# One weight product of a decoder layer computed as seven block products per pair of output tiles

## The reference

```
h  = rmsnorm(x) ; z = h @ W_in                          # values, gates, q, k, v
c  = silu(layernorm(causal_conv31(val * sigmoid(glu))))
ya = ((c @ w_pw) * silu(c_gate)) @ w_br_conv            # convolution branch
yb = (attention(q, k, v) * silu(a_gate)) @ w_br_attn    # attention branch
m  = sigmoid(g_conv) * ya + sigmoid(g_attn) * yb
x  = x + rmsnorm(m @ w_out) ; x = x + sigmoid(x @ w_pg) * (p @ w_pp)
```

## Time and profile before

| | |
|---|---|
| median of 3 runs (1166.1 to 1166.4) | 1166.13 us |
| span of the profiled execution | 1164.1 us |
| median above that span | 2.0 us |
| PE busy | 1158.8 us, 100% |
| DVE busy | 856.9 us, 74% |
| ACT busy | 377.5 us, 32% |

### The profile page before, as it was taken

One profiled execution on the slowest core, in us unless ns is written; L12 is line 12 of the kernel. 1 busy time (PEld: TensorE's weight loads), 2 busy tenths in 40 slices (PEclk: granted clock), 3 DMA queues, 4 the chain that ended last, 5 costly groups with the idle time before them and its releaser, 6 DMA issues.

```text
span 1164.1 us, 16101 instructions
## 1 busy us (share of the span) xinstructions
PE 1158.8 (100%) x6304; PEld 945.5 (81%) x6304; DVE 856.9 (74%) x961; ACT 377.5 (32%) x671; POOL 18.0 (2%) x16
## 2 busy tenths in 40 slices
PE   9999999999999999999999999999999999999998
PEld 7888888888888888877777888888888888888887
DVE  6999999999999984699986688683233344357776
ACT  6431221221221221366665442441112112344342
POOL 2020000000000000000000000000000000000000
PEclk9999999999999999999999999999999999999999
DMA  9622122122222323211112111333232232434565
GB/s 352 274 90 72 60 84 72 63 81 72 67 78 72 100 54 86 54 56 56 58 56 77 50 55 37 108 108 96 85 108 92 88 108 81 136 113 141 174 205 180
DMA packets 35675, 116.42 MB, mean 100 GB/s; under 512 B 4496, under 2 KB 5264, under 8 KB 35632
## 3 DMA queue, kind: packets, MB, share of 16 engines
q1 hardware_dynamic: 25264, 82.29, 21.3%
q10 hardware_dynamic: 10368, 33.56, 8.3%
HBM read 92.10 MB, written 20.97 MB: 97 GB/s over the span
## 4 chain that ended last, share of the span: by engine, by line
PE 97%; DVE 1%; ACT 1%; DMA 0%; issue 0%; SPq 0%; ACTq 0%; DVEq 0%
PE psg L470 81%; PE psg L762 6%; PE psg L494 2%; PE psb L676 1%; PE psg L733 1%; PE psg L577 1%; PE psg L523 1%; PE psg L694 1%; ACT probs L1009 1%; PE psg L728 1%; PE psb L577 1%; PE psg L819 0%; DMA p_raw<-pT 0%; DVE smax L1471 0%; DVE probs L1495 0%; DVE probs L1465 0%
## 5 line engine op out<-in xcount | busy, mean ns | idle before, releaser
L470 PE MATMUL psg<-h_hi,w_hi 128*128 128x512 f32 x768 | 236.9, 390 | 0.0
L470 PE MATMUL psg<-h_hi,w_lo 128*128 128x512 f32 x768 | 236.5, 389 | 0.0
L470 PE MATMUL psg<-h_lo,w_hi 128*128 128x512 f32 x768 | 236.4, 389 | 0.0
L1213 DVE TENSOR_TENSOR w_lo<-w_raw,w_hi 128x1024 fp32r<-128x1024 f32 x113 | 138.1, 1222 | 89.1 <-ACT w_hi L865 85.4
L865 ACT ACTIVATE w_hi<-w_raw 128x1024 fp32r<-128x1024 f32 x112 | 118.5, 1058 | 250.4 <-PE psg L470 230.7
L470 PEld LDWEIGHTS psg<-h_hi,w_lo 128*128 128x128 f32 x768 | 144.1, 188 | 30.1
L470 PEld LDWEIGHTS psg<-h_hi,w_hi 128*128 128x128 f32 x768 | 143.8, 188 | 30.4 <-issue 0.8
L470 PEld LDWEIGHTS psg<-h_lo,w_hi 128*128 128x128 f32 x768 | 144.1, 188 | 30.0
L1390 DVE SCALAR_TENSOR_TENSOR conv<-u,cols,conv 128x1024 f32<-128x1024 f32 x120 | 154.1, 1284 | 0.0
L1390 DVE SCALAR_TENSOR_TENSOR work<-u,cols,work 128x1024 f32<-128x1024 f32 x112 | 145.5, 1300 | 0.0
L762 PE MATMUL psg<-h_hi,w_hi 128*128 128x512 f32 x128 | 51.8, 405 | 0.0
(11 more groups left out here) (257 smaller groups left out, 1763.2 us busy)
## 6 DMA issues: line engine op xcount, KB each, us to landing
w_raw<-weights SPq DMA_DIRECT2D x114, 512.0 KB, 3.4
gates<-ring ACTq DMA_DIRECT2D x24, 512.0 KB, 2.7
ring<-gates ACTq DMA_DIRECT2D x24, 512.0 KB, 3.4
x_rows<-x_rows SPq DMA_DIRECT2D x8, 512.0 KB, 10.1
conv<-xT SPq DMA_DIRECT2D x8, 512.0 KB, 14.3
ple<-ple_out SPq DMA_DIRECT2D x8, 512.0 KB, 13.5
x_ring<-xT ACTq DMA_DIRECT2D x16, 256.0 KB, 3.5
ple_all<-ple ACTq DMA_DIRECT2D x8, 512.0 KB, 4.7
```

Of the source, the lines that this page charges most:

```text
L470: mm = nc.tensor.matmul(psg[:, slot, h * HALF:(h + 1) * HALF], w[:, wslot, (wk + k) * P:(wk + k + 1) * P], r[:, k, h * HALF:(h + 1) * HALF ...
L1213: nc.vector.tensor_tensor(w_lo[:, slot, :], w_raw[:, slot, :], w_hi[:, slot, :].bitcast(F32), ALU.subtract).then_inc(w_lo_ready, 1)
```

## The change

F's numbers vanish and G, H, I move down by eight (`G0` = 66). The product `c @ w_pw` is done for four **pairs** of output tiles. For a pair the operands are seen as 2 x 2 blocks: `c` by halves of the features (4 row tiles) and halves of the 1024 columns, the weights by halves of the features and the two output tiles. Plain multiplication takes eight block products, each of 4 k-steps x 3 passes = 12 matmuls of 128x512. The new code uses Winograd's form with seven, named P1, P2, P6, Q5, P7, Q3, P4 in the order in which PE does them (`seventh`). It needs

- four sums of blocks of `conv` (`row_sum`, s blocks 0 to 3), each 128x2048, with their high part (`sum_high`, ACT) and low part (`row_low`, DVE), once for all pairs;
- per pair four sums of weight blocks (`pair_sum`, DVE, 128x512), and for each of the seven products a high part (`block_high`, ACT) and a low part (`block_low`, DVE), in six slots of `pair_w`, which lie over `w_raw`, `w_hi` and `w_lo`;
- per pair four copies out of PSUM (`keep`, ACT): P6, P7, Q3 and P4 are added onto a bank that holds earlier products, so PE waits for the copy (`kept_ready`) before it goes on there;
- per pair four quarters of the result (`take`, DVE): an add or subtract and a product with the gate, all of 128x512 (the last of them the product alone). Rows of y are then split after the third pair (`y_high`, `y_low`).

The s blocks lie over `o_lo` and `o_hi`, which PE reads until the end of tile 65; `o_used` frees them in quarters. `merged` is no longer kept in SBUF: DVE writes each row to `merged_out` (`merge_row`), ACT sends it to memory (`spill_merged`), and SP loads the eight rows back during the last pair and after (`merged_back`). The normalisation is done by the fifth E tile that DVE reads out (`norm_beside`).

Core of the diff (`...` marks what is left out):

```diff
-            return ((0,), (1, 2), (3,), (4, 5), (6,), (7,), (), ())[m]
+            return ((0, 1), (2,), (3, 4), (5,), (6, 7), (), (), ())[m]
...
+            sp.wait_ge(product_made, LAST_PAIR)
+            load_tile(G0)
...
+            for k in range(4):
+                merged_back(k)
+            sp.wait_ge(product_made, LAST_PAIR + 7)
+            load_tile(G0 + 1)
+            for k in range(4, KT):
+                merged_back(k)
...
-            pairs(F0, G0, c_hi, c_lo, 2 * KT)
...
+            def seventh(i, n):
+
+                b = 7 * i + n
...
+                pe.wait_ge(pair_lo, b + 1)
...
+                if i == 0 and n in (P6, P7, Q3):
+                    pe.wait_ge(s_ready, {P6: 2, P7: 3, Q3: 4}[n])
...
+                if onto:
+                    pe.wait_ge(kept_ready, 4 * i + {P6: 1, P7: 2, Q3: 3, P4: 4}[n])
...
+            block_high(0)
+            block_high(1)
+            sum_high(0)
+            sum_high(1)
+            block_high(2)
+            sum_high(2)
+            block_high(3)
+            keep(0, P1)
+            sum_high(3)
+            block_high(4)
+            block_high(5)
+            keep(0, P6)
+            keep(0, Q5)
+            block_high(6)
+            load_gate(KT + 1, 1, G0 // 2)
+            spill_merged(KT - 1)
+            for b in range(7, 7 * PAIRS):
+                for i, n in made_since(b):
+                    if n in (P1, P6, Q5, P7) and 7 * i + n > Q5:
+                        keep(i, n)
...
+                block_high(b)
+            y_high(0)
+            y_high(1)
+            keep(PAIRS - 1, P7)
+            high(G0 // 2 - 1, 2)
+            for k in range(2, KT):
+                y_high(k)
+            high(G0 // 2 - 1, 3)
...
+                if n < 3:
+                    dve.wait_ge(o_used, n + 1)
...
+                nc.vector.tensor_tensor(s_raw[:, n], a, b, op).then_inc(s_made, 1)
```

More of the change, by code:

```diff
@@ L55 @@
 E0 = 58
[L56 to L61, removed]
+G0 = 66
+H0 = 74
+I0 = 90
+TILES = 106
+WTILES = 90
+PAIRS = KT // 2
+KP = KT // 2
+P1, P2, P6, Q5, P7, Q3, P4 = range(7)
+LAST_PAIR = 7 * (PAIRS - 1)
 PLE_STEPS = 2
@@ L134, in build @@
         w_lo = at("w_lo", [2, KT * P], F32R, W + 16 * KB)
+        pair_w = at("pair_w", [6, 2, HALF], F32R, W)
+        pair_t = at("pair_t", [6, 2, HALF], F32, W)
         tanh_t = at("tanh_t", [S], F32, G)
@@ L346, in norm_beside, with pair_slot, slot_before, pair_bank @@
         def norm_beside(m):
-            return ((0,), (1, 2), (3,), (4, 5), (6,), (7,), (), ())[m]
+            return ((0, 1), (2,), (3, 4), (5,), (6, 7), (), (), ())[m]
+        def pair_slot(b):
+            r = b % 6 if b < LAST_PAIR else 3 + (b - LAST_PAIR) % 3
+            return 2 * r if r < 3 else 2 * (r - 3) + 1
+        def slot_before(b):
+            if b < 6:
+                return None
+            return b - 6 if b < LAST_PAIR + 3 else b - 3
+        def pair_bank(i, n):
+            return {P2: 2, Q5: 3, Q3: 3}.get(n, i % 2)
+        def made_since(b):
+            first = 2 if b == 7 else slot_before(b - 1) + 1
+            return [divmod(c, 7) for c in range(first, slot_before(b) + 1)]
+        def from_slot(eng, b):
+            if b < 6:
+                eng.wait_ge(tile_done, G0 - 1 + KT + (b >= 3))
+            else:
+                eng.wait_ge(product_made, slot_before(b) + 1)
         block = ctx.enter_context(nc.Block())
@@ L799, in _ @@
             pairs(D0 + 6, E0, h_hi, h_lo)
-            pairs(E0, F0, o_hi, o_lo, KT)
-            pairs(F0, G0, c_hi, c_lo, 2 * KT)
+            pairs(E0, G0 - 2, o_hi, o_lo, KT)
+            tile(G0 // 2 - 1, 0, o_hi, o_lo)
+            pe.wait_ge(w_lo_ready, G0 - 1 + PLE_STEPS + 1)
+            pe.wait_ge(ps_free[1], G0 // 2 + 3)
+            for k in range(KT):
+                for n, (w, r) in enumerate(((w_hi, o_hi), (w_lo, o_hi), (w_hi, o_lo))):
+                    for h in range(2):
+                        mm = nc.tensor.matmul(psg[:, 1, h * HALF:(h + 1) * HALF], w[:, 1, k * P:(k + 1) * P],
+                                              r[:, k, h * HALF:(h + 1) * HALF],
+                                              start=(k == 0 and n == 0), stop=(k == KT - 1 and n == 2))
+                if k % 2 == 1 and k < KT - 1:
+                    mm.then_inc(o_used, 1)
@@ L802, in _ @@
+            for i in range(PAIRS):
+                for n in range(7):
+                    seventh(i, n)
             pairs(G0, H0, y_hi, y_lo, 3 * KT)
@@ L1118, in _ @@
                 load_gate(m, j, a2)
+                if m >= 2:
+                    spill_merged(m - 2)
                 if m == 0:
@@ L1124, in _ @@
                         c_high(k - 1)
-                high(a2, j + 2)
-                if m == KT - 1:
+                if m < KT - 2:
+                    high(a2, j + 2)
+                if m == 5:
                     c_high(KT - 1)
[L1128 to L1135, removed]
+            load_gate(KT, 0, G0 // 2)
+            spill_merged(KT - 2)
+            block_high(0)
[18 more added lines that the diff above has]
+                        keep(i, n)
+                    if n == P1 and i > 0:
+                        act.wait_ge(y_made, 4 * i)
+                        for j in range(2):
+                            act.dma_start(ring[:, j, :], GATES[:, KT + 2 * i + j, :]).then_inc(gate_loaded[j], 16)
+                block_high(b)
[6 more added lines that the diff above has]
+            high(G0 // 2 - 1, 3)
+            act.wait_ge(y_made, 4 * PAIRS)
             with act.Fori(0, KT // 2) as i:
@@ L1628, in gate, with merge_row, pair_sum @@
                 dve.wait_ge(gate_loaded[j], r * 16)
-            for m in range(KT):
+            def merge_row(m):
                 a2, j = (E0 + m) // 2, m % 2
+                gate(a2, j, m // 2 + 1)
+                if m >= 2:
+                    dve.wait_ge(merged_spilled[j], 16 * (m // 2))
+                stt(merged_out[:, j, :], ring[:, j, :], 1.0, psg[:, j, :], ALU.add, ALU.mult).then_inc(ps_free[j], 1)
+            def pair_sum(i, n):
+                blocks = pair_raw[i % 2]
+                dve.wait_ge(pair_loaded[i % 2], 16 * (i // 2 + 1))
+                if n == Q5:
+                    out, a, b = pair_sums[:, 0, :], blocks[:, 0, :], blocks[:, 1, :]
+                elif n == P6:
+                    dve.wait_ge(pair_summed, 4 * i + 1)
+                    out, a, b = pair_sums[:, 1, :], pair_sums[:, 0, :], blocks[:, 3, :]
+                elif n == P4:
+                    from_slot(dve, 7 * i + n)
+                    out, a, b = pair_t[:, pair_slot(7 * i + n), 1, :], pair_sums[:, 1, :], blocks[:, 2, :]
+                else:
+                    from_slot(dve, 7 * i + n)
+                    out, a, b = pair_t[:, pair_slot(7 * i + n), 1, :], blocks[:, 1, :], blocks[:, 3, :]
+                nc.vector.tensor_tensor(out, a, b, ALU.add).then_inc(pair_summed, 1)
@@ new lines, in _, with row_sum @@
+            upper, lower = slice(0, HALF), slice(HALF, S)
+            def row_sum(n):
+                a11, a12 = conv[:, 0:KP, upper], conv[:, KP:, upper]
+                a21, a22 = conv[:, 0:KP, lower], conv[:, KP:, lower]
+                if n < 3:
+                    dve.wait_ge(o_used, n + 1)
+                else:
+                    dve.wait_ge(tile_done, G0 + KT)
+                if 0 < n < 3:
+                    dve.wait_ge(s_made, n)
+                a, b, op = ((a21, a22, ALU.subtract), (s_raw[:, 0], a11, ALU.subtract),
+                            (a12, s_raw[:, 1], ALU.add), (a11, a21, ALU.subtract))[n]
+                nc.vector.tensor_tensor(s_raw[:, n], a, b, op).then_inc(s_made, 1)
@@ new lines, in row_low, with take @@
+            def row_low(n):
+                dve.wait_ge(s_hi_ready, n + 1)
+                stt(s_lo[:, n], s_raw[:, n], 0.5, s_hi[:, n].bitcast(F32), ALU.mult, ALU.subtract).then_inc(s_ready, 1)
+            def take(i, n):
+                m, half = ((2 * i, upper), (2 * i + 1, lower), (2 * i + 1, upper), (2 * i, lower))[n]
+                dve.wait_ge(product_made, 7 * i + (P2, P7, Q3, P4)[n] + 1)
+                if n > 0 or i > 0:
+                    dve.wait_ge(y_made, 4 * i + n)
+                if n < 3:
+                    dve.wait_ge(kept_ready, 4 * i + (1, 4, 2)[n])
+                    a, b, op = ((psb[:, pair_bank(i, P2), :], kept[:, 0, :], ALU.add), (kept_q5[:], kept[:, 0, :], ALU.subtract),
+                                (psb[:, pair_bank(i, Q3), :], kept[:, 1, :], ALU.subtract))[n]
+                    nc.vector.tensor_tensor(quarter[:], a, b, op).then_inc(quarter_read, 1)
+                    dve.wait_ge(quarter_read, 3 * i + n + 1)
+                dve.wait_ge(gate_loaded[m % 2], (i + 5) * 16)
+                nc.vector.tensor_tensor(y_raw[:, m, half], quarter[:] if n < 3 else psb[:, pair_bank(i, P4), :],
+                                        ring[:, m % 2, half], ALU.mult).then_inc(y_made, 1)
@@ L1632, in _, with y_low @@
+            def y_low(k):
```

(61 more changed lines are left out.)

133 lines of the change are left out of this document (119 added, 14 removed).

## The result

The changed kernel takes 1169.14 us (median of 11 runs, 1168.2 to 1170.5) against 1166.20 of the kernel before: a ratio of 1.0024 with an interval of 1.0016 to 1.0032, slower by 0.24%. The profiled execution has a span of 1167.3 us, 3.2 more than before.

The account below looks back on a forecast made before the run. PE's list of matmuls was taken to bound the kernel. -10.9 + 0.1 + 1.5 + 0.1 + 5.2 + 2.9 = -1.1 us gave a span of 1163.0, with 2.0 for the median 1165.0 us; range 1161.8 to 1169.5.

Parts of the forecast that it names:

- What is removed: In the product done in pairs, 48 fewer matmuls at 0.2266 us each: 10.9 us less on PE.
- The prices: Costs of added operations, such as 2.28 us on DVE and 1.92 us on ACT for 128x2048.
- The entry: From tile 65's end to P4 of pair 0: PE loses 0.1, 1.5 (before P7), 0.1 and 5.2 us (before P4).
- The exit: From the last product to tile 66: PE waits 2.9 us for the low part of tile 66's weights.
- Steady state: Second to fourth pair: DVE's 11.7 and ACT's 6.9 us hide beside PE's 19.0 us per pair; no loss.
- normalisation: In E, done in five tiles instead of eight: DVE's 46.7 of 54.4 us, hidden.
- merged rows: Eight spills and eight loads of 512 KB share the DMA engines; DVE waits for them, nothing reaches PE.
- The sum: Over the whole kernel, the gain and PE's waits add to -1.1 us: span 1163.0, time 1165.0 us.
- the forecast's own case: Whole kernel with entry and exit waits as worked out: 1165.0 us, bounds 1163.2 to 1167.7, chance 63%.
- the clock falls: Rival: idle of 5.2 us before P4 drops PE's clock to 1.2 GHz, giving 1167.7 to 1170.5 us; chance 12%.
- a falling clock as a sign of being wrong: Behind the copy keep(0, P7) before P4: the forecast is wrong if the granted clock falls after it.
- 11 were named as a sign: Whole kernel: PE's busy time lower by 11 us, with 48 fewer matmuls, would show the forecast right.

Follow-up runs that it names:

- Run 1: Changed kernel with the copy of P7 (pair 0) right behind ACT's last high part of pair 0 and take(0, 0) before row_low(3) on DVE: 1166.39 us.
- Run 2: Changed kernel with high and low part of tile 66's weights moved ahead of y_high(0) and y_low(0): 1164.72 us.
- run 4: Changed kernel with thrown-away matmuls on PE, 20 before P4 of pair 0 and 10 before tile 66: 1165.27 us.
- run 7: Kernel before, with PE held ahead of tile 66 (first of F) while GpSimd fills a free tile five times: 1174.66 us.
- run 8: Kernel before, with PE held ahead of tile 66 (first of F) while GpSimd fills a free tile twice: 1170.67 us.
- run 3: Changed kernel with the moves of run 1 and Run 2 together: 1162.97 us.
- run 6: Changed kernel with only the 20 thrown-away matmuls before P4 of pair 0, the wait before tile 66 left in: 1166.63 us.
- run 5: Changed kernel with the moves of run 1 and Run 2, plus ACT's copy of P1 (pair 1) before the high part of that pair's P7: 1159.55 us.

## Why the prediction was wrong, point by point

**What is removed, 10.9 us: right.** Outside the waits and the slow stretches, 21 products take 57.16 us, 0.2269 us per matmul.

**The prices: right.** In the trace after, the 128x2048 operations take 2.29 us on DVE and 1.92 to 1.93 on ACT, where 2.28 and 1.92 were estimated. Here is ACT at the entry, with the copy of P7 at 832.99:

```profile
817.82 1.92 ACT L1262 ACTIVATE s_hi<-s_raw 128x2048 fp32r<-128x2048 f32 x1 [2.08 <-DVE s_raw L1881]
...
828.69 0.33 ACTq L1225 DMA_DIRECT2D ring<-gates  x1
829.05 0.46 ACTq L1245 DMA_DIRECT2D merged<-merged_out  x1
829.61 1.15 ACT L1257 ACTIVATE pair_w<-pair_raw 128x512 fp32r<-128x512 f32 x2 [2.81 <-DVE merged_out L1836]
832.45 0.63 ACT L1257 ACTIVATE pair_w<-pair_sums 128x512 fp32r<-128x512 f32 x1 [1.70 <-DVE pair_sums L1853]
832.99 0.58 ACT L1272 ACTIVATE kept<-psb 128x512 f32<-128x512 f32 x1
```

**The entry: right.** 0.1 us lost before P6 (forecast 0.1), 1.3 before P7 (1.5), 5.3 before P4 (5.2), by the steps that were named. The chain is the one forecast: gate load behind the read-out of tile 65, three high parts, the last behind two sums, then the copy. Run 1 confirms the cause and adds what the prediction didn't say: ACT's list holds a second copy of this kind, P1 of pair 1, hidden behind the first.

**The exit: right.** 2.9 us lost (2.9). DVE has two y_low at 890.27 and two at 893.60, then the `take` in two operations, and `w_lo` only 1.4 us after the products had ended at 895.77:

```profile
893.60 2.36 DVE L1418 SCALAR_TENSOR_TENSOR y_lo<-y_raw,y_hi 128x1024 fp32r<-128x1024 f32 x2 [0.97 <-ACT y_hi L1279]
895.88 0.68 DVE L1898 TENSOR_TENSOR quarter<-kept_q,kept 128x512 f32<-128x512 f32 x1
896.60 0.69 DVE L1901 TENSOR_TENSOR y_raw<-quarter,ring 128x512 f32<-128x512 f32 x1
897.20 1.22 DVE L1409 TENSOR_TENSOR w_lo<-w_raw,w_hi 128x1024 fp32r<-128x1024 f32 x1
```

Run 2 confirms it.

**Steady state, normalisation, merged rows: right.** 0.1 us is lost in 21 products; P1 starts at 810.33, 0.1 us after F did before; once tile 66 has begun PE waits for nothing in G, H and I, and H and I take the same 179.9 us. DVE does wait for the merged rows before it reads out tile 66, until 911.98, some 0.7 us after PE has ended that tile, and as forecast nothing of it reaches PE. One size in that part was wrong without a consequence: the eight spills of 512 KB are 4.2 MB, not 2.1.

**The sum: here the prediction failed.** "-10.9 + 0.1 + 1.5 + 0.1 + 5.2 + 2.9 = -1.1 us" takes every wait at its own length and puts the clock at nothing. The three waits were forecast at 9.6 us and measured at 9.5; with the small pieces it is 9.8 against 10.1. So the sum would have been right had the granted clock stayed at 1.00 "throughout": run 4, in which it did, takes 1165.27 us against the forecast 1165.0. The term for the clock is 3.9 us: 2.2 behind P4's wait, 1.7 behind the one at the exit. The time of 1169.14 us is thus 4.1 above the forecast and slower than before where a little faster was expected; that it still lies inside the stated range is no merit of the forecast's own case, whose long end was 1167.7.

The prediction had the mechanism as the rival "the clock falls" and named a falling clock as a sign of being wrong. But it gave the rival 12% and looked only at the longer wait. The trace of before had no idle above 1.3 us in it, so its granted clock of 1.00 was no evidence on idles of 5.2 and 2.9 us, and no other row spoke against the rival. Its price for one fall, 12 to 24 matmuls at twice their time or 2.7 to 5.4 us, was too high: the falls cost 2.2 and 1.7 us, with ten slow matmuls in P4 and eight behind the exit, at 0.42 to 0.43 us each. Both together lie inside it, which is luck. PE's busy time fell by 6.1 us (1158.8 to 1152.7, with 48 matmuls fewer) where 11 were named as a sign: a matmul at the lower clock counts as busy for longer. The Trainium skill (TensorE: Matmul & The Clock Gate, Part 1) says that the clock goes to half after idle and comes back with sustained activity. The runs agree: the clock is at 0.50 behind 5.3 us (changed kernel) and 5.6 us (run 7) of idle, and back near 1.00 from 837.7 and 821.0 on; behind those of 2.9 and 2.6 us (changed kernel, run 8) it fell only after PE's return. That rule should have carried most of the chance.

**Left open.** In pair 0, P1 and P2 run at 0.2266 us per matmul, but P6 and Q5 take 5.57 us and P7 and Q3 5.66 where 5.44 is usual, and 0.1 us stands before P6; no run looked at it. What decides whether an idle of 2.9 us brings the clock down in a given execution was not found either.

## What to carry to other kernels

Where TensorE has hardly waited before, a change that saves matmuls can pay twice for a new wait: the wait itself, and behind waits of 2.6 to 5.6 us, as they came in these runs, 1.7 to 2.2 us of half clock. So at the seams between stages it is worth ordering ACT's and DVE's lists by when TensorE needs each result: two moved copies, one moved `take` and one moved weight split turned +0.24% into -0.59% with the same arithmetic. After such a repair, look at the next instruction of the same kind in the same list; in run 1 the wait moved there. When runs of one program scatter by more than 0.2%, compare their mean granted clock first; it sorted the executions of runs 1, 3 and 6, but not those of the changed kernel, where those at 0.997 (1168.2 to 1169.9 us) and those at 0.995 or 0.996 (1168.7 to 1170.5) overlap.

## What the runs showed that was not expected

The clock can fall after TensorE has come back: in the changed kernel 0.9 us, in run 6 1.0 us and in run 8 0.7 us after its return from 2.9, 2.9 and 2.6 us of idle. A wait of this size doesn't always do it (run 6, by the mean clock: no in five of eleven executions, yes in six), so a kernel with such waits can have a spread of its own: 3.2 us in run 6, 4.3 in run 3, 5.1 in run 1. Without waits above 1.6 us the spread is 1.3 to 1.9 us in the three sets of the kernel before (11 to 29 runs), 1.9 in run 4 with a mean clock of 1.000 in all eleven, and 0.4 in run 5 (5 runs); the 2.2 us of the changed kernel stand out little from that. Useless matmuls in a wait can make a kernel faster, by 3.9 us in run 4.
